# A two-block model kernel: first-layer rows moved to the second layer's end, x loaded in quarters, an eight-tile last norm in a mixed form

## What is computed

```python
# first block (once)
h = rms_norm(x, norm1_w);  z = h @ w_in                     # 8192 columns: u, q, k, v, two gates
y_ssm  = s5_mixer(z[u], ...);  y_attn = diff_attention(z[q], z[k], z[v], ...)   # q and k are rms-normed
m = sigmoid(z[gs]) * (y_ssm @ w_proj_ssm) + sigmoid(z[ga]) * (y_attn @ w_proj_attn)
x = x + m @ w_out
x = x + (silu(h2 @ w_ffn_gate) * (h2 @ w_ffn_up)) @ w_ffn_down     # h2 = rms_norm(x, norm2_w)
# second block, two layers l = 0, 1
u = x @ w_in_2[l]                                           # conv branch, MLA, RWKV-7 branch
mix = concat(y_conv, y_mla, y_rwkv)
x = layer_norm(4 ** 0.25 * x + mix @ w_out_2[l], ln_g[l], ln_b[l])
```

## Time and profile before

| | |
|---|---|
| median of 3 runs | 2410.68 us (2409.13 to 2410.85) |
| the profiled execution, its own time | 2409.45 us |
| its span | 2407.6 us |
| matmuls busy (PE) | 2343.2 us, 97% |
| VectorE, ScalarE, GpSimd busy | 1456.2, 1143.8, 197.7 us |
| mean granted TensorE clock | 0.994 |

### The profile page before, as it was taken

One profiled execution on the slowest core, in us unless ns is written; L12 is line 12 of the kernel. 1 busy time (PEld: TensorE's weight loads), 2 busy tenths in 40 slices (PEclk: granted clock), 3 DMA queues, 4 the chain that ended last, 5 costly groups with the idle time before them and its releaser, 6 DMA issues.

```text
span 2407.6 us, 38790 instructions
## 1 busy us (share of the span) xinstructions
PE 2343.2 (97%) x16401; PEld 2027.6 (84%) x16401; DVE 1456.2 (60%) x1788; ACT 1143.8 (48%) x1598; POOL 197.7 (8%) x200
## 2 busy tenths in 40 slices
PE   7999999999999999999999999999999999999997
PEld 7777777888888888888888899889898898899985
DVE  4999956756554554554444446745755568456556
ACT  5676656644454444444433434433554545334542
POOL 4000000002000000000000001310000151301000
PEclk9999999999999999999999999999999999999998
DMA  8554555565566666666555575334547674335465
GB/s 240 172 162 154 160 189 157 159 199 179 187 189 192 184 188 189 192 188 190 190 192 192 187 224 173 115 98 123 165 132 243 174 215 136 98 107 158 140 208 168
DMA packets 260365, 415.76 MB, mean 173 GB/s; under 512 B 53448, under 2 KB 74440, under 8 KB 259424
## 3 DMA queue, kind: packets, MB, share of 16 engines
q1 hardware_dynamic: 254496, 395.63, 54.1%
q0 software_dynamic: 5376, 17.56, 2.5%
q10 hardware_dynamic: 320, 0.08, 0.0%
HBM read 406.90 MB, written 7.87 MB: 172 GB/s over the span
## 4 chain that ended last, share of the span: by engine, by line
PE 88%; DVE 8%; ACT 2%; issue 2%; DMA 0%; ACTq 0%; SPq 0%; DVEq 0%
PE banks L585 86%; DVE wp_hl L1166 2%; ACT wp_hl L1844 1%; DVE r_SA L1684 0%; PE banks L697 0%; PE banks L709 0%; PE banks L822 0%; ACT L1844 0%; DMA xt<-x 0%; DVE r_SA L1650 0%; DVE rsd L1290 0%; DVE nsd L1543 0%; DVE r_kb L1652 0%; DVE xr L1837 0%; DVE xr L1835 0%
## 5 line engine op out<-in xcount | busy, mean ns | idle before, releaser
L1166 DVE TENSOR_TENSOR wp_hl<-raw,wp_hl 128x1024 fp32r<-128x1024 f32 x740 | 915.7, 1244 | 858.8 <-ACT wp_hl L1844 857.9
L1844 ACT ACTIVATE wp_hl<-raw 128x1024 fp32r<-128x1024 f32 x740 | 782.1, 1060 | 1076.9 <-PE banks L585 1055.5
L585 PE MATMUL banks<-wp_hl,XX_hl 128*128 128x512 f32 x3840 | 899.3, 394 | 5.2 <-DVE wp_hl L1166 5.2
L585 PEld LDWEIGHTS banks<-wp_hl,XX_hl 128*128 128x128 f32 x3840 | 719.2, 189 | 165.6 <-issue 11.0
L585 PE MATMUL banks<-XX_hl,wp_hl 128*128 128x256 f32 x4992 | 644.0, 287 | 9.6 <-DVE wp_hl L1166 7.4
L585 PEld LDWEIGHTS banks<-XX_hl,wp_hl 128*128 128x128 f32 x4992 | 609.2, 192 | 27.8 <-issue 14.1
L585 PE MATMUL banks<-wp_hl,FF_hl 128*128 128x512 f32 x1056 | 240.6, 390 | 0.0
L585 PEld LDWEIGHTS banks<-wp_hl,FF_hl 128*128 128x128 f32 x1056 | 198.1, 188 | 40.7
L585 PE MATMUL banks<-wp_hl,MXa_hl 128*128 128x512 f32 x384 | 88.3, 389 | 0.0
L585 PE MATMUL banks<-wp_hl,MM_hl 128*128 128x512 f32 x384 | 88.3, 391 | 0.0
L585 PEld LDWEIGHTS banks<-wp_hl,MXa_hl 128*128 128x128 f32 x384 | 72.1, 188 | 14.9
(11 more groups left out here) (439 smaller groups left out, 1776.6 us busy)
## 6 DMA issues: line engine op xcount, KB each, us to landing
raw<-w_in SPq DMA_DIRECT2D x304, 512.0 KB, 3.8
raw<-w_out SPq DMA_DIRECT2D x96, 512.0 KB, 4.5
raw<-w_ffn_gate SPq DMA_DIRECT2D x88, 512.0 KB, 3.7
raw<-w_ffn_up SPq DMA_DIRECT2D x88, 512.0 KB, 3.7
raw<-w_ffn_down SPq DMA_DIRECT2D x88, 512.0 KB, 3.6
raw<-w_proj_attn SPq DMA_DIRECT2D x16, 512.0 KB, 4.2
raw<-w_proj_ssm SPq DMA_DIRECT2D x16, 512.0 KB, 3.6
raw<-w_glu SPq DMA_DIRECT2D x8, 512.0 KB, 3.8
```

Source lines behind the costliest of these rows:

```text
L585: return e.matmul(o, lhsT, rhs, start=start, stop=stop, skip_group_check=True)
L1166: return tt(d, src, hi, SUB)
L1844: return e.activation(o, x, func, bias=bias, scale=scale)
```

## The change

1. x is loaded in four quarters of its columns, between the first pieces. It is turned as it is, by a plain transpose; 1/rms comes in behind the products. `u` is multiplied in its evacuation by a row of 1/rms (`rsd`, a product of `dg` with ones, copied by ScalarE), both banks on VectorE; v and the gates take it as a scale per token; the q and k sums take it in two small steps (t = 11 and 13). The squares move into the ten turns, the roots into turn 8.
2. The S5 loads are put between later pieces (constants ahead of piece 5, `ssm_c` ahead of 9 and 11, `ssm_b` ahead of 13 and 15, the rest ahead of 17).
3. `kept[1]` holds the normed `xr`, without gain and bias. The 16 operations of GpSimd go, and so do layer 0's loads of gain and bias. In layer 1 GpSimd loads, for each column block, `xr`, gain and bias of layer 0 (`first_rows`) and of layer 1, and VectorE applies layer 0's (`kept_rows`, four operations of 128x512 for each block).
4. The last norm: for column blocks 0 to 2 `x * lng` is made right after the statistics. At the end TensorE makes `lnb - mean * rstd * lng` in a bank by two products of four rows (`crow`, `G4`), so that each of these six tiles takes one operation. Block 3 goes first, in the form of before. `G4` is a rounded copy and a remainder of four rows of 2048, made on ScalarE and VectorE during `xo11` and `xo21`.

```diff
-    cols("u", 2, w1, 0, 16, "AV")
+    cols("u", 2, w1, 0, 16, "VV")
...
 SP
+        quarter(0)
+        weights(0)
+        weights(1)
+        quarter(1)
+        weights(2)
+        weights(3)
+        quarter(2)
+        quarter(3)
...
+            if p == 5:
+                e.dma_start(cst[:, 128:COLS_AT], A["consts"][:, 128:COLS_AT]).then_inc(s_s5, 16)
+            elif p in (13, 15):
+                d, name = (br, "ssm_b_re") if p == 13 else (bi, "ssm_b_im")
...
+            elif p in (9, 11):
...
 TensorE, turned_x and entered
             if stage == 0:
-                e.wait_ge(*XD("d", stage))
+                e.wait_ge(s_x[g // 2], 32)
...
-                    if stage == 0:
-                        last = mm(B[b][:, o:o + 128], src, dg[:, 128 * t:128 * t + 128], o == 0, o == 384)
-                    else:
-                        last = e.transpose(B[b][:, o:o + 128], src, ident)
+                    last = e.transpose(B[b][:, o:o + 128], src, ident)
...
+                if stage == 0 and g == 9:
+                    bank(6, *XR("r"))
+                    e.wait_ge(*XD("d"))
+                    mm(B[6][:, 0:256], M["ones"], dg, True, True).then_inc(XRP.made("p"), 1)
...
 TensorE, at the end
+        e.wait_ge(*FIN("c"))
+        emptied(e, "cb1")
+        for q in range(4):
+            last = e.transpose(B[4][0:4, 128 * q:128 * q + 128], endc[:, q // 2, q % 2, :].bitcast(F32), ident)
+        last.then_inc(FNT.made("t"), 1)
+        e.wait_ge(*FNA("r"))
+        e.wait_ge(*FIN("l"))
+        for n, (c, t) in enumerate(ENDING[2:]):
+            if n > 2:
+                e.wait_ge(*OUT("o", n - 1))
+            w = slice(512 * c, 512 * c + 512)
+            mm(B[5 + n % 3], crow[0:4, 128 * t:128 * t + 128], G4.h[0:4, w], True, False)
+            mm(B[5 + n % 3], crow[0:4, 256 + 128 * t:384 + 128 * t], G4.l[0:4, w], False, True).then_inc(FNW.made("w", n), 1)
...
 VectorE, evac
-                e.tensor_copy(pair(dst, 2 * c + 1), b[1]).then_inc(s_evV, 1)
+            if n == "u":
+                e.wait_ge(*XR("r"))
+                for i in range(2):
+                    tt(uT[:, 4 * int(l) + 2 * i:4 * int(l) + 2 * i + 2, :], v3(b[i], 2), wide3(rsd, 2, 256), MUL).then_inc(s_evV, 1)
...
                     e.bn_stats(bns[:, 6 * m:6 * m + 6], xr[:, i, 512 * c:512 * c + 512]).then_inc(LNS.made("b", 8 * l + 2 * c + i), 1)
+                    if l and c < 3:
+                        e.wait_ge(*LNS("b", 8 * l + 2 * c + i))
+                        tt(x, x, lng[:, 512 * c:512 * c + 512], MUL).then_inc(LXG.made("g", 2 * c + i), 1)
...
+        def kept_rows(c):
+            main(at.until(f"xo{c - 1}1" if c else "cb1"))
+            main(at.go(6))
+            e.wait_ge(s_xr[c], 16 * 6)
+            for op, i in ((MUL, 0), (ADD, 1)):
+                for t in range(2):
+                    if i:
+                        e.wait_ge(*YM("m", 2 * c + t))
+                    x = xr[:, t, 512 * c:512 * c + 512]
+                    last = tt(x, x, first_rows[c % 2][:, 512 * i:512 * i + 512], op)
...
+                kept_rows(0)
+                kept_rows(1)
+                main(at.go(4))
+                for k in range(4):
+                    last = e.memset(endc[:, :, :, k].bitcast(F32), 1.0 if k == 1 else 0.0)
+                last.then_inc(FIN.made("one"), 1)
+                e.wait_ge(*FNA("g"))
+                lo(G4.l[0:4, :], g4[0:4, :], G4.hi_f(0, 2048)[0:4, :]).then_inc(FIN.made("l"), 1)
+                kept_rows(2)
+                kept_rows(3)
             main(at.until(f"xo3{l}"))
...
 ScalarE
             main(at.until(f"cb{l}"))
             at.limit(f"xo3{l}")
+            if l:
+                main(at.until(f"xo1{l}"))
+                e.wait_ge(s_gb2, 64)
+                hi(G4.h[0:4, :], g4[0:4, :]).then_inc(FNA.made("g"), 1)
             main(at.until(f"xo2{l}"))
...
+        e.wait_ge(*FNT("t"))
+        act(crow[0:4, :], B[4][0:4, :], ACT.Copy).then_inc(FNA.made("r"), 1)
...
 GpSimd
+            if l:
+                e.wait_ge(*over("cb1"))
+                for i, name in enumerate(("ln_g_2", "ln_b_2") * 2):
+                    e.dma_start(g4[i:i + 1, :], A[name][1:2, :]).then_inc(s_gb2, 16)
...
+                if l:
+                    if c > 1:
+                        e.wait_ge(*YA("b", 2 * c - 3))
+                    for i, name in enumerate(("ln_g_2", "ln_b_2")):
+                        e.dma_start(first_rows[c % 2][:, 512 * i:512 * i + 512], A[name][0, w].partition_broadcast(128)).then_inc(s_xr[c], 16)
...
-                for m in range(8):
-                    c, t = m // 2, m % 2
-                    w = slice(512 * c, 512 * c + 512)
-                    tt(xt[:, t, w], xr[:, t, w], lng[:, w], MUL).then_inc(YT.made("m", m), 1)
-                    e.wait_ge(*YT("m", m))
-                    tt(xt[:, t, w], xt[:, t, w], lnb[:, w], ADD).then_inc(YT.made("b", m), 1)
-                e.wait_ge(*YT("b", 7))
-                e.dma_start(tokens(kept[1]), xt).then_inc(s_kept, 16)
+                e.wait_ge(*LX("x", 7))
+                e.dma_start(tokens(kept[1]), xr).then_inc(s_kept, 16)
```

More of the change, by code:

```diff
@@ L368, in program @@
     xr, lng, lnb = v3(alloc("xr", 4096), 2), alloc("lng", 2048), alloc("lnb", 2048)
+    first_rows = [alloc("first_rows0", 1024)]
+    assert at[0] <= OWN
+    at[0] = OWN + 4096
+    first_rows.append(alloc("first_rows1", 1024))
+    assert at[0] <= ARENA - 1024
+    at[0] = XX_AT
+    g4, ends, crow = alloc("g4", 2048), alloc("ends", 8), place("crow", 512, F32R)[:, :]
+    G4 = Pair("G4", 2048)
+    endc = place("endc", 16, F32R)[:, :].rearrange("p (s t k) -> p s t k", s=2, t=2)
     jobs = []
@@ L526, in _, with quarter @@
     def _(e):
-        for h in range(2):
+        def quarter(c):
+            w = slice(512 * c, 512 * c + 512)
             for t in range(2):
-                c = slice(1024 * h, 1024 * h + 1024)
-                e.dma_start(xt[:, t, c], A["x"][0, 128 * t:128 * t + 128, c]).then_inc(s_x[h], 16)
+                e.dma_start(xt[:, t, w], A["x"][0, 128 * t:128 * t + 128, w]).then_inc(s_x[c], 16)
         def weights(p):
@@ L567, in _ @@
             weights(p)
-        for m in range(8):
-            c, t = m // 2, m % 2
+        for m, (c, t) in enumerate(ENDING):
             e.wait_ge(*OUT("o", m))
@@ L1345, in _ @@
                 rest_of_x(0, g)
+            if g == 0:
+                split(0)
+            elif g == 8:
+                roots(0)
             if g > 1:
@@ L1431, in _ @@
         e.wait_ge(*SV("im"))
+        main(at.share(1.95))
         for d, x in zip(BP, (m3, m4)):
@@ L1435, in _ @@
         last.then_inc(SV.made("bp"), 1)
-        main(at.share(1.95))
         main(at.until("u1"))
@@ L1472, in _ @@
                 s_result(t - 1)
-            if t == 13:
-                e.wait_ge(*DQ("s"))
-                e.reciprocal(qkn, qkn).then_inc(DR.made("r"), 1)
+            of_half = lambda i: qkn.rearrange("p (z i x) -> p i z x", z=2, i=2)[:, i]
+            if t == 11:
+                e.wait_ge(*DA("q", 7))
+                for i in range(2):
+                    last = ts(of_half(i), of_half(i), rs[:, 2 + i:3 + i], rs[:, 2 + i:3 + i], MUL, MUL)
+                last.then_inc(DR.made("x"), 1)
+            elif t == 13:
+                e.wait_ge(*DQ("s"))
+                e.reciprocal(qkn, qkn).then_inc(DR.made("c"), 1)
+                e.wait_ge(*DR("c"))
+                for i in range(2):
+                    last = ts(of_half(i), of_half(i), rs[:, 2 + i:3 + i], None, MUL)
+                last.then_inc(DR.made("r"), 1)
             e.wait_ge(*ROT("zi", t))
@@ L1889, in evac @@
             b = [B[x] for x in j.banks]
[L1890 removed]
+            if n not in ("u", "pa", "ps", "wo", "fd", "rk", "rv", "rr", "ch", "cb") and n[:2] not in ("fu", "xo"):
                 e.wait_ge(*over(j.name))
[L1892 to L1894 removed]
+            if n in ("cq", "cc", "pq"):
                 act(pair({"cq": cq, "cc": cu, "pq": qp}[n], 0), b[0], ACT.Copy).then_inc(s_evA, 1)
@@ L2004, in _ @@
                 rounded_x(0, g)
+            if g == 0:
+                split(0)
+            if g < 8:
+                c, t = g // 2, g % 2
+                e.wait_ge(s_x[c], 32)
+                squares(0, 4 * t + c, g, xt[:, t, 512 * c:512 * c + 512])
+            elif g == 8:
+                e.wait_ge(s_ones, 32)
+                roots(0)
+            else:
+                e.wait_ge(*XRP("p"))
+                act(rsd, B[6][:, 0:256], ACT.Copy).then_inc(XR.made("r"), 1)
             if g > 1:
```

108 lines of the change are left out of this document (52 added, 56 removed).

## The result

The changed kernel takes **2415.9 us** in the median of 16 runs (2412.7 to 2420.1), the kernel before 2410.6 (16 runs, 2408.3 to 2412.5). The ratio is 1.0023 with a 95% interval of 1.0016 to 1.0030: slower by 5.3 us, which is little, but the interval leaves out 1. It stands within the predicted range of 2402.5 to 2416.5, 4.0 above the predicted 2411.9. The profiled execution took 2419.74, with a span of 2417.9, 3.8 above the median. Its stalls are read here for their causes; sizes come from medians of runs, further down.

The account below looks back on a forecast made before the run. TensorE was taken to bound the kernel, its matmuls busy 97% of the span. Head -4.2, boundary -0.3, tail -3.3 and G4 +9.05 give +1.2, so 2410.68 becomes 2411.9 us, range 2402.5 to 2416.5.

Parts of the forecast that it names:

- head: Start of the kernel to the end of `u0` and the next wait: 4.2 us gained, 2.5 to 6.5.
- tail: Last norm after the last job: six tiles of one operation each gain 3.3 us, bounds 2.5 to 4.2.
- G4: End of `xo11`: TensorE idles 6.7 us for G4's rounding and loses 2.35 to the clock; 9.05, bounds 8.1 to 9.9.
- kept rows with the boundary: Second layer's kept rows cost nothing; GpSimd's operations leaving the layer boundary gain 0.3 us, 0 to 0.7.
- Cost nothing; bound 0 to 1.2: End of the second layer: VectorE's wait for row loads and its added work are covered by ready pieces.
- late rows: Rival: four groups' loads land about 11 us after issue, past the cover; +5.2 us, 2417.1; chance 0.15.
- the cover of 1.8: First column block of kept rows: 1.8 us of VectorE's waiting for loads is hidden before TensorE stands.
- the clock's loss: Head: the first weight matmuls run at half clock, costing 2.4 us, within 1.4 to 3.2.
- the roots' wait: Head, group 8: TensorE waits 0.8 us for the roots and spends 0.4 on the row product.
- GpSimd's work at the boundary: Layer boundary: GpSimd's 16 operations go, gaining 0.3 us, 0 to 0.7.
- The rival built on it (3.8): Layer boundary: the stretching of four VectorE splits is on the path, 3.8 us gained; 2408.4; chance 0.04.
- SP's loads priced at nothing: Head: ssm_b and ssm_c loads between weights cost nothing, as four raw buffers cover them; without cover up to 4 us.

Follow-up runs that it names:

- e5: e3 with the last norm as before the change, so that only the head is left of it: 2403.0 us, ratio 0.9967 to the kernel before.
- e3: The changed kernel with G4 rounded earlier on ScalarE and layer 0's gain and bias applied by GpSimd as before: 2400.6 us, ratio 0.9956 to the kernel before.
- e1: The changed kernel with only ScalarE's rounding of G4 moved earlier, to ten steps into xo11: 2406.1 us, ratio 0.9980 to the kernel before.
- e2: The changed kernel with only the kept rows undone, layer 0's gain and bias applied by GpSimd as before: 2410.3 us, ratio 1.0001 to the kernel before.
- e6: e3 with the two first_rows loads issued again for each column block, read by nobody: 2400.3 us, ratio 0.9958 to the kernel before.
- e12: e6 plus VectorE's four operations for each block on operands already there, waiting only for xr: 2400.4 us, ratio 0.9956 to the kernel before.
- e7: e6 with the two added loads reading 128 rows that lie apart instead of one row 128 times: 2402.2 us, ratio 0.9961 to the kernel before.
- e10: The change with G4 rounded earlier, kept rows waiting for three transfers and fewer loads, but S5 loads placed as before the change: 2410.8 us, ratio 1.0003.

## Why the prediction was right in its range and wrong in a term

| term | predicted | measured (medians) | from |
|---|---|---|---|
| head | -4.2 | -7.9 | e5 against before |
| tail | -3.3 | -2.5 | e3 against e5 |
| G4 | +9.05 | +9.8 | change against e1; e2 against e3 gives 9.7 |
| kept rows with the boundary | 0 - 0.3 | +5.6 | change against e2; e1 against e3 gives 5.5 |
| sum | +1.2 | +5.0 (measured directly: +5.3) | |

*The step that failed* is "Cost nothing; bound 0 to 1.2" for the kept rows. The rival "late rows" came true, beside the G4 stall and not instead of it. Its condition, landings of about 11 us after issue, was met at the first block (11.4). Its price, 5.2, is close to the 5.6 by luck: it was 1.3 at each of four blocks, while in e1 TensorE loses 4.3 at the first (2.39 of waiting, the rest at the lower clock behind it), 1.2 at the third and 0.4 at the last. The gap in the working is the landing. I put the fifth load's landing at 7.3 and some 2 more; it was 10.4 in the median and 11.4 where it mattered. On the clock of the kernel before, 2316.1 and the 4.2 gained are 2320.3, 2.8 to 4.3 behind my 2316 to 2317.5. VectorE's arrival, 2310.26, is the forecast 2314.6 less the 4.2 gained, so its lateness of 5.90 less the cover of 1.8 gives 4.1, and TensorE waited 3.84. Who waits for whom and the cover were right, the landing was not. I also asked only who waits for the rows: e6 shows that the same five transfers hold back the weights by 3.5 to 5 us at every block. That was a gap too, but a cheap one, at 1.0 us in e6's profile and nothing in e12's, where VectorE's work is there as well.

*The mis-sized term* is the head. Trace against trace, the first product was 0.4 earlier than the 11.8, the clock's loss 1.5 (4.62 for 3.11) instead of 2.4, the roots' wait 0.87 as worked out. 6.2 were gained there instead of 5.0, and 0.6 of it was given back at the next wait. The rest up to 7.9 is how the profiled execution of before stands to its median (1.2), and what five or six runs can't resolve: e5's span is 6.4 shorter than that of before.

*Right by its own steps:* G4 (idle 6.54 against 6.7, clock 2.6 against 2.35) and its cause, the place in ScalarE's queue. The tail's form, with six operations of VectorE in 5.01 us, 0.85 apart for the forecast 0.87. GpSimd's work at the boundary, 0.5 of TensorE's time in the trace (TensorE's second piece at the boundary comes 3.7 earlier than before, `xo01` 4.2) against 0.3. The rule of the Trainium skill on the shared port pair ("SBUF — State Buffer") agrees with the trace: with GpSimd silent each remainder takes 1.23, where four took 8.66 beside it. The rival built on it (3.8) is refuted, as VectorE had slack there.

*SP's loads priced at nothing* held as put: in the trace TensorE waits for none of the moved loads. I weighed only what the new places risk ("up to 4") and not what the old ones would have cost. That is 11.4, and the head's gain rests on it.

That the total came within the range is in part luck: the head's extra 3.7 paid for most of the rows. Some two thirds of the chance lay between 2405.9 and 2415.5, within 0.2% of before; the measured 2415.9 (1.0023) lies just beyond that edge, which is also the upper end of the forecast's own 2408 to 2415.5.

## What to carry to other kernels

Count the transfers that a wait covers, and wait only for those that the next instruction reads: one semaphore for five loads made work wait for data that was needed some 14 us later (ten steps at 2.72 us for two), or never. Where a burst of small loads goes past a stream, price what it does to the stream first (how many ready pieces it uses up), and have other work done ahead of the gap, where e12 shows it to be free. When two engines hand a side product to each other, put both at the same step of their queues: six steps apart cost 9.8 us for 4.2 us of work. And moving slow loads out of the start can be what an earlier start hangs on (11.4 us here).

## What the runs showed of the hardware that was not expected

- A burst of loads by GpSimd's queue, each a row of 2 KB read by 128 partitions, shuts out SP's weights for a while. In the change SP issues pieces at 2307.55, 2308.69 and 2310.28, and from 2309 to 2312 the DMA engines are busy 0.88 of the time at 149 GB/s with not one packet of weights. Before, the same stretch moved 231 GB/s at 0.86. With two of the four broadcast rows replaced by rows that lie apart (e7), ScalarE's waits for weights are 2.6 to 3.2 us instead of 3.5 to 5.0.
- The two loads of `ssm_b_re`, in rows of 64 bytes, hold SP's queue for 8.26 us in a burst behind other loads (e10), and for 3.31 (e5) to 6.58 us (the change) between pieces of weights.
- TensorE's first products run slower (24 matmuls in 4.62, then 3.11) while the granted clock is shown as 1.00.
- After the same wait of 4.35 us at the layer boundary the clock falls for the next piece in some executions and not in others: 24 matmuls take 3.11 us in three of the fourteen profiled executions and 4.65 to 5.45 in eleven.
